# Cache attention of a decoder step: a mirrored key weight in place of eight score columns

## The chip, the cores and the metric

One core of a Trainium2 chip runs the whole program. The metric is the device time of one execution in microseconds (us), as a median over runs. PE is TensorE (PEld its weight loads), DVE is VectorE, ACT is ScalarE, POOL is GpSimd, SP is SyncE, whose queue issues most transfers.

## What is computed

One layer of a decoder for 1024 prompt tokens and 8 sequences with one new token each (decode tokens). Every decode sequence has 8192 earlier positions in a paged cache: a latent of 256 values and a rotary key of 32 values. The part that matters here, cut from the reference (`qf` is the normed query of 8 heads x 96 values, 64 of them without rotary part):

```python
def mla_keys(ckv, kpe, w_uk, g_kn):
    k_nope = jnp.einsum('btc,chd->bthd', ckv, w_uk)
    k_pe = jnp.broadcast_to(kpe[:, :, None, :], ...)
    return rms_norm(jnp.concatenate([k_nope, k_pe], axis=-1), qk_gain(g_kn))
...
k = mla_keys(ckv_blk, kpe_blk, w_uk, g_kn)
s = jnp.einsum('bqhd,bkhd->bhqk', qf, k) * scale
...
p = jnp.exp(s - m_new[..., None])
acc = acc * alpha[..., None] + jnp.einsum('bhqk,bkc->bhqc', p, ckv_blk)
```

So for each cached position two things are needed of the 8 x 64 key values k = latent x w_uk: their squares' sum per head (for the norm) and their product with the query per head (the score). The rotary part adds 32 more values, shared by the heads.

## The kernel before

The program is a row of stages, each a block in which the five engines run their own instruction streams and wait for each other on semaphores: `project_in`, `make_heads`, `attend_prompt` (attention of the prompt), `cache_and_merge` (the cache attention of the 8 sequences, then the output projection with w_o and the norm), `gate_and_up`, `down` (the MLP). Wide products are made at fp32 accuracy with three fp32r products: an operand is split into `hi` (rounded) and `lo` (rest), and hi x hi, hi x lo and lo x hi are added in PSUM.

`cache_and_merge` goes through the 8 sequences one after the other. A sequence has 64 tiles of 128 positions, taken as 32 pairs `n`. `gather` on POOL issues indirect loads, two per chunk of 8 tiles (latents of 1 MB, rotary keys), two sequences ahead. For each pair:

- PE, `turn`: four transposes of the next pair's latents into `TT`. ACT copies them as `hi` (L1498), DVE makes `lo` (L1667).
- PE, `keys` (L1306 to L1318): for each of the two tiles 6 products (2 halves of the latent, `ck`, x 3 terms) with the key weights. The weights `w_hi`, `w_lo` have 520 columns: 512 of w_uk and 8 that hold w_uk x query, so that the scores fall out beside the key values. A PSUM bank takes 512 fp32 columns, so each product is two matmuls of 260 columns, `half` 0 and 1, into two banks: 12 matmuls a tile, 24 a pair.
- ACT, `squares` (L1591): squares of the 512 key values from `KK` in PSUM into `sq` in SBUF.
- DVE, `sums`: sums of 64 squares for each head out of `sq` (L1769), then a copy of the 8 scores out of `KK` (L1771), which increments `scored`.
- `KK` has room for two tiles. `keys` of tile t waits for `scored` of tile t-2 (L1310 to L1311):

```python
for t in range(2):
    if n >= 1 or b > 0:
        pe.wait_ge(scored, b * TILES + 2 * n + t - 1)
```

The order of the work is written by hand. On PE a pair is: rotary transposes if n % 4 == 0 (`turn_rotary`), `turn(n + 1)`, `keys(n)`, rotary product if n % 4 == 1 (`rotary`). On DVE it is: `lo(n)`, at n == 24 `queries`, `sums(n - 1)`, `rotary_scores` if n % 4 == 3 (L1776, L1780), then a step of the softmax tail of the sequence before (`tail`, n = 9, 11, 13, 17, 21). On ACT: `hi(n)`, `squares(n - 1)`, `rotary_turned` if n % 4 == 0. In the last sequence ACT and DVE also split w_o (L1526, L1689) in pairs 19 to 31.

`queries` (L1647 to L1659) puts the next sequence's 8 score columns into `w_hi` and `w_lo` (4 small operations) and its rotary query into `q_pe` (1). Before the first sequence, PE multiplies w_uk with all queries (L1468, "absorbed"), ACT and DVE split the result (L1617, L1834).

## Time and profile before

| | |
|---|---|
| median of 3 runs | 2309.01 us (2308.57 to 2309.56) |
| profiled execution, own time | 2308.62 us |
| its span | 2306.8 us |
| cache stage, from the first `keys` to the last | 432 to 1382 us |
| mean granted TensorE clock | 0.984 of full |

The span is the time from the first to the last instruction of the profiled execution; its own time is 1.8 us longer and 0.4 us under the median. A row of a timeline is start, duration, engine, line, operation, output <- input, shapes, and in brackets the idle time before it with what ended it. Rows with xN are N instructions merged; then the duration runs from the first start to the last end. Matmuls are pipelined: one starts before the end of the one before it, so the spacing of starts tells their price, not their duration.

### The profile page before, as it was taken

The page shows a single profiled execution, that of the slowest core. Times are in us where ns is not written, and L with a number is a line of the kernel's source. Part 1 is how long each engine was busy: PE and PEld are TensorE (multiplying, and loading weights), DVE is VectorE, ACT ScalarE, POOL GpSimd, SP SyncE. Part 2 cuts the span into 40 slices and gives each one's busy share as a digit, 9 for nine tenths or more (in the row PEclk, how much of TensorE's full clock was granted, in tenths as well). Part 3 has the DMA queues.
Part 4 walks back from the last instruction along what each step waited for, and adds up shares of the span by engine and source line. Part 5 has one row for each costly group of instructions (what it writes and reads, how often), then busy time and mean ns, then how long its engine had stood idle before and what let it go on. Part 6 is the DMA issues. An engine that isn't in the chain of part 4 may idle for free. (4 is left out here: it accounts for less than half of the span.)

```text
span 2306.8 us, 39961 instructions
## 1 busy us (share of the span) xinstructions
PE 2240.1 (97%) x15923; PEld 2009.7 (87%) x15923; DVE 1393.4 (60%) x2663; ACT 946.9 (41%) x1788; POOL 325.5 (14%) x412
## 2 busy tenths in 40 slices
PE   8989899899999999999999999989999999999998
PEld 7965466799999999999999987769999999978776
DVE  4326677566666666666666675556767676754345
ACT  4435566455454545454545563321111111133334
POOL 2106300501212212130303112100000000000000
PEclk9989999899999999999999999999999999999999
DMA  4110000710212212030404014221111111144444
GB/s 158 48 40 0 39 19 11 291 58 1 110 57 79 88 51 116 24 142 4 163 1 174 11 55 148 75 77 46 45 45 45 45 45 45 37 140 127 165 168 134
DMA packets 93449, 180.39 MB, mean 78 GB/s; under 512 B 9048, under 2 KB 64168, under 8 KB 84927
## 3 DMA queue, kind: packets, MB, share of 16 engines
q1 hardware_dynamic: 77789, 93.65, 12.7%
q0 software_dynamic: 15504, 84.60, 9.5%
q8 instruction: 105, 1.72, 0.3%
q14 instruction: 51, 0.42, 0.1%
HBM read 164.21 MB, written 14.33 MB: 77 GB/s over the span
## 5 line engine op out<-in xcount | busy, mean ns | idle before, releaser
L1769 DVE TENSOR_REDUCE ca_cells<-ca_sq 128x8 f32<-128x512 f32 x512 | 350.8, 685 | 257.7 <-ACT ca_sq L1591 255.0
L1591 ACT ACTIVATE ca_sq<-ca_KK 128x512 f32<-128x512 f32 x512 | 306.6, 599 | 382.5 <-PE ca_KK L1315 382.4
L1315 PE MATMUL ca_KK<-ca_w_hi,ca_hi 128*128 128x260 f32 x2048 | 432.2, 292 | 1.9 <-DVE ca_cells L1771 1.5
L1315 PE MATMUL ca_KK<-ca_w_lo,ca_hi 128*128 128x260 f32 x2048 | 412.5, 283 | 0.0
L1315 PE MATMUL ca_KK<-ca_w_hi,ca_lo 128*128 128x260 f32 x2048 | 412.3, 283 | 0.0
L1315 PEld LDWEIGHTS ca_KK<-ca_w_hi,ca_hi 128*128 128x128 f32 x2048 | 313.6, 189 | 4.6 <-issue 2.8
L1315 PEld LDWEIGHTS ca_KK<-ca_w_lo,ca_hi 128*128 128x128 f32 x2048 | 316.1, 189 | 0.0
L1315 PEld LDWEIGHTS ca_KK<-ca_w_hi,ca_lo 128*128 128x128 f32 x2048 | 315.3, 189 | 0.0
L1940 PE MATMUL gu_GU<-mlp_h_hi,gu_w_hi 128*128 128x344 f32 x1056 | 225.1, 322 | 3.2 <-DVE gu_w_lo L1985 3.2
L1667 DVE TENSOR_TENSOR ca_lo<-ca_TT,ca_hi 128x512 fp32r<-128x512 f32 x256 | 175.6, 686 | 82.6 <-ACT ca_hi L1498 75.7
L1940 PE MATMUL gu_GU<-mlp_h_lo,gu_w_hi 128*128 128x344 f32 x1056 | 224.7, 321 | 0.0
L1940 PE MATMUL gu_GU<-mlp_h_hi,gu_w_lo 128*128 128x344 f32 x1056 | 223.4, 320 | 0.0
L1498 ACT ACTIVATE ca_hi<-ca_TT 128x512 fp32r<-128x512 f32 x256 | 152.7, 597 | 74.0 <-PE ca_TT L1290 73.9
L1940 PEld LDWEIGHTS gu_GU<-mlp_h_hi,gu_w_hi 128*128 128x128 f32 x1056 | 178.4, 189 | 3.3 <-DVE gu_w_lo L1985 3.3
L1940 PEld LDWEIGHTS gu_GU<-mlp_h_lo,gu_w_hi 128*128 128x128 f32 x1056 | 179.5, 190 | 0.0
L1940 PEld LDWEIGHTS gu_GU<-mlp_h_hi,gu_w_lo 128*128 128x128 f32 x1056 | 176.3, 188 | 0.0
L1290 PE MATMUL ca_TT<-keep_ident,ca_lat 128*128 128x128 f32 x1024 | 155.2, 274 | 0.9 <-issue 0.9
L2026 DVE RECIPROCAL gu_room<-gu_room 128x1032 f32<-128x1032 f32 x22 | 145.3, 6603 | 0.8
L1290 PEld LDWEIGHTS ca_TT<-keep_ident,ca_lat 128*128 128x128 f32 x1024 | 119.7, 142 | 4.2 <-issue 4.0
L1966 ACT ACTIVATE gu_room<-gu_GU 128x1032 f32<-128x1032 f32 x22 | 22.8, 1036 | 226.1 <-PE gu_GU L1940 226.1
L2171 PE MATMUL dn_OUT<-dn_w_hi,dn_g_hi 128*128 128x512 f32 x352 | 111.6, 398 | 1.2 <-DVE dn_g_lo L2230 0.3
L2227 DVE TENSOR_TENSOR dn_w_lo<-dn_raw,dn_w_hi 128x1024 fp32r<-128x1024 f32 x44 | 53.9, 1225 | 93.5 <-ACT dn_w_hi L2193 93.5
(309 smaller groups left out, 3297.9 us busy)
## 6 DMA issues: line engine op xcount, KB each, us to landing
dn_raw<-in_w_down SPq DMA_DIRECT2D x44, 512.0 KB, 3.7
keep_w_uv<-in_w_gate SPq DMA_DIRECT2D x22, 512.0 KB, 3.8
gu_up_raw<-in_w_up SPq DMA_DIRECT2D x22, 512.0 KB, 3.9
keep_ctx<-in_w_down SPq DMA_DIRECT2D x22, 512.0 KB, 3.7
late_room<-in_x_prompt SPq DMA_DIRECT2D x8, 512.0 KB, 3.7
ca_m<-mixed_scratch SPq DMA_DIRECT2D x8, 512.0 KB, 4.0
ca_w_raw<-in_w_o SPq DMA_DIRECT2D x16, 256.0 KB, 2.7
ca_x<-in_x_prompt SPq DMA_DIRECT2D x8, 512.0 KB, 3.7
```

What stands on the lines that cost most here:

```text
L1290: last = nc.tensor.transpose(TT[:, n % 2, (2 * t + ck) * P:(2 * t + ck + 1) * P], src, keep.ident[:])
L1315: last = nc.tensor.matmul(KK[:, t, half, 0:HALF], x[:, n % 2, t, ck, :], w[:, ck, half, par * (NH // 2):par * (NH // 2) + HALF], start=(m ...
L1498: nc.scalar.activation(hi[:, n % 2], TT[:, n % 2, :].rearrange("p (t c k) -> p t c k", t=2, c=2), ACT.Copy).then_inc(hi_done, 1)
L1591: nc.scalar.activation(sq[:, t], KK[:, t, :, KEYS[par]], ACT.Square).then_inc(squared, 1)
L1667: nc.vector.tensor_tensor(lo[:, n % 2], TT[:, n % 2, :].rearrange("p (t c k) -> p t c k", t=2, c=2), hi[:, n % 2].bitcast(F32), ALU.subtra ...
L1769: nc.vector.tensor_reduce(ss[:, par, 2 * n + t, :], sq[:, t].rearrange("p a (h d) -> p (a h) d", d=DN), AX.X, ALU.add).then_inc(summed, 1)
L1940: ins = nc.tensor.matmul(GU[:, 3 * kind + j, 0:F3], w[:, kind, k, :], h[:, k, j * F3:(j + 1) * F3], start=(k == 0 and n == 0), stop=(k == ...
L1966: nc.scalar.activation(gate[:, 2:2 + TOK].rearrange("p (j t) -> p j t", j=3), GU[:, 0:3, 0:F3], ACT.Copy)\
L2026: link(nc.vector.reciprocal(sig, sig))
L2171: last = nc.tensor.matmul(OUT[:, t, h, :], g[:, b, t * P:(t + 1) * P], w[:, b, h * 512:(h + 1) * 512], start=(f == 0 and k == 0), stop=(f ...
L2227: nc.vector.tensor_tensor(w_lo[:, b, :], raw[m % RING], w_hi[:, b, :].bitcast(F32), ALU.subtract).then_inc(w_lo_done, 1)
```

## The change

The 8 score columns go. For each sequence and head, the 64 columns of w_uk are multiplied by a reflection (a "mirror") that takes the first axis to the direction of the head's query. A reflection keeps the sum of squares, so the norm can be taken from the mirrored key values, and the first of them is, up to a factor `coef`, the score. Weights are then 512 columns wide, one bank, but differ from sequence to sequence.

- `keys` issues 6 matmuls of 512 columns a tile. `KK` and the new `SQ` are banks of one PSUM tensor `KS`: ACT now squares from PSUM into PSUM, DVE reduces from PSUM. The copy of the 8 scores becomes a product with `coef`, read with a step of 64.
- New per sequence: SP loads a row of 512 values, broadcast to 128 partitions (`w_row`, 256 KB, from a scratch in DRAM). DVE, `refresh`: `fresh = w_row * u`, then `fresh += w_uk`, for each of two `ck`, in pairs 20 and 22. ACT, `split_w`: `w_hi = fresh` in pairs 23 and 25. DVE, `refresh_lo`: `w_lo = fresh - w_hi` in pairs 24 and 27. `queries` keeps 1 of its 5 operations.
- New once: 9 DVE operations at the end of `make_heads` (8 partitions), which also loses the two query units (8 transposes, 2 ACT copies) at its end; 17 POOL operations and 2 stores in `attend_prompt`, 4 small ACT operations there, after items 14 and 30 of 64; 8 transposes and an ACT copy before "absorbed". Before the first sequence, `refresh`, `split_w` and `refresh_lo` of sequence 0 stand on the way; the old split of w_uk (2 ACT, 2 DVE operations) is gone.
- The rotary keys of two sequences no longer fit and lie in a ring of 12 chunks: `gather` waits on POOL for `kpe_squared` from the 5th chunk on.

```diff
@@ make_heads, DVE, at its end
+            q = keep.q_s[:, :, 0:DN]
+            big, none, ge = (keep.mirror[:, n, :] for n in (BIG, NONE, SIGN))
+            step(nc.vector.tensor_reduce(big, q, AX.X, ALU.max, apply_absolute_value=True))
...
+            step(nc.vector.tensor_reduce(keep.mirror[:, SQUARE, :], keep.w_row, AX.X, ALU.add))
@@ attend_prompt, ACT
+                if n == 14:
+                    guess_norm()
+                if n == 30:
+                    guess_inverse()
@@ places in a sequence
+FRESH_AT, HI_AT, LO_AT = (20, 22), (23, 25), (24, 27)
@@ gather, POOL
+        if b >= 1 and n >= RING - CHUNKS:
+            nc.gpsimd.wait_ge(keep.kpe_squared, (b - 1) * CHUNKS + n - (RING - CHUNKS) + 1)
@@ PSUM
-        KK = c.ps("KK", [P, 2, 2, 512])
+        KS = c.ps("KS", [P, 2, 2, 512])
+        KK, SQ = KS[:, :, 0, :], KS[:, :, 1, :]
@@ SP
+            for b in range(NB):
+                if b >= 1:
+                    sp.wait_ge(w_made, 2 * b)
+                if b >= 2:
+                    sp.wait_ge(complete, b - 1)
+                sp.dma_start(w_row, row_broadcast(keep.w_dram[b:b + 1, :], WIDE)).then_inc(w_in, 16)
@@ PE, keys
-                        for half in range(2):
-                            last = nc.tensor.matmul(KK[:, t, half, 0:HALF], x[:, n % 2, t, ck, :],
-                                                    w[:, ck, half, par * (NH // 2):par * (NH // 2) + HALF],
-                                                    start=(m == 0), stop=(m == 5))
+                        last = nc.tensor.matmul(KK[:, t, :], x[:, n % 2, t, ck, :], w[:, par, ck, :],
+                                                start=(m == 0), stop=(m == 5))
@@ ACT, squares, and the new split
-                    nc.scalar.activation(sq[:, t], KK[:, t, :, KEYS[par]], ACT.Square).then_inc(squared, 1)
+                    nc.scalar.activation(SQ[:, t, :], KK[:, t, :], ACT.Square).then_inc(squared, 1)
+            def split_w(b, ck):
+                act.wait_ge(w_made, 2 * b + ck + 1)
+                nc.scalar.activation(w_hi[:, b % 2, ck, :], fresh[:, b % 2, ck, :], ACT.Copy).then_inc(w_hi_set, 1)
@@ DVE
+            def refresh(b, ck):
+                if ck == 0:
+                    dve.wait_ge(w_in, 16 * (b + 1))
+                    if b > 1:
+                        dve.wait_ge(keyed, b * TILES - TILES)
+                new = fresh[:, b % 2, ck, :].rearrange("p (h d) -> p h d", h=NH)
+                made = nc.vector.tensor_tensor(new, w_row.rearrange("p (h d) -> p h d", h=NH),
+                                               keep.u[:, ck, b, :].unsqueeze(2).to_broadcast([P, NH, DN]), ALU.mult)
+                made.then_inc(w_step, 1)
+                dve.wait_ge(w_step, 2 * b + ck + 1)
+                nc.vector.tensor_tensor(fresh[:, b % 2, ck, :], fresh[:, b % 2, ck, :], keep.w_uk[:, ck, :], ALU.add)\
+                  .then_inc(w_made, 1)
+            def refresh_lo(b, ck):
+                dve.wait_ge(w_hi_set, 2 * b + ck + 1)
+                last = nc.vector.tensor_tensor(w_lo[:, b % 2, ck, :], fresh[:, b % 2, ck, :],
+                                               w_hi[:, b % 2, ck, :].bitcast(F32), ALU.subtract)
+                if ck == 1:
+                    last.then_inc(q_set, 1)
@@ DVE, sequence, after lo(n) and ahead of sums(n - 1)
-                    if n == 24 and b < NB - 1:
+                    if n in FRESH_AT and b < NB - 1:
+                        refresh(b + 1, FRESH_AT.index(n))
+                    if n == LO_AT[0] and b < NB - 1:
                         queries(1 - par, b + 1)
+                    if n in LO_AT and b < NB - 1:
+                        refresh_lo(b + 1, LO_AT.index(n))
@@ DVE, sums
-                    nc.vector.tensor_reduce(ss[:, par, 2 * n + t, :], sq[:, t].rearrange("p a (h d) -> p (a h) d", d=DN),
+                    nc.vector.tensor_reduce(ss[:, par, 2 * n + t, :], SQ[:, t, :].rearrange("p (h d) -> p h d", d=DN),
                                             AX.X, ALU.add).then_inc(summed, 1)
-                    nc.vector.tensor_copy(raw[:, par, 2 * n + t, :].rearrange("p (a h) -> p a h", a=2),
-                                          KK[:, t, :, SCORES[par]]).then_inc(scored, 1)
+                    nc.vector.tensor_tensor(raw[:, par, 2 * n + t, :], KK[:, t, :].rearrange("p (h d) -> p h d", d=DN)[:, :, 0],
+                                            keep.coef[:, b, :], ALU.mult).then_inc(scored, 1)
```

How the order moves, on PE, in the middle of a sequence: the first tile of a pair before (`ca_KK` are the key products, `ca_TT` the transposes of the next latents).

```order
L1290 MATMUL ca_TT<-keep_ident,ca_lat 128x128 x4
L1315 MATMUL ca_KK<-ca_w_hi,ca_hi 128x260 x2
L1315 MATMUL ca_KK<-ca_w_lo,ca_hi 128x260 x2
L1315 MATMUL ca_KK<-ca_w_hi,ca_lo 128x260 x2
L1315 MATMUL ca_KK<-ca_w_hi,ca_hi 128x260 x2
L1315 MATMUL ca_KK<-ca_w_lo,ca_hi 128x260 x2
L1315 MATMUL ca_KK<-ca_w_hi,ca_lo 128x260 x2
```

And the same tile in the changed program:

```order
L1366 MATMUL ca_TT<-keep_ident,ca_lat 128x128 x4
L1390 MATMUL ca_KS<-ca_w_hi,ca_hi 128x512
L1390 MATMUL ca_KS<-ca_w_lo,ca_hi 128x512
L1390 MATMUL ca_KS<-ca_w_hi,ca_lo 128x512
L1390 MATMUL ca_KS<-ca_w_hi,ca_hi 128x512
L1390 MATMUL ca_KS<-ca_w_lo,ca_hi 128x512
L1390 MATMUL ca_KS<-ca_w_hi,ca_lo 128x512
```

Twelve instructions of a tile have become six; the second tile of the pair follows in the same way.

On DVE of the changed program, pairs 19 to 20 of a sequence (`ca_fresh` is the new weight, `ca_cells` takes sums and scores):

```order
L1876 COPY ca_cells<-ca_KP 128x64
L1880 TENSOR_REDUCE ca_cells<-ca_kpe_sq 128x8
L1763 TENSOR_TENSOR ca_lo<-ca_TT,ca_hi 128x512
L1735 TENSOR_TENSOR ca_fresh<-keep_w_uv,attn_u 128x512
L1739 TENSOR_TENSOR ca_fresh<-ca_fresh,attn_w_uk 128x512
L1869 TENSOR_REDUCE ca_cells<-ca_KS 128x8
L1871 TENSOR_TENSOR ca_cells<-ca_KS,attn_coef 128x8
```

The two rows L1735 and L1739 are new, between `lo(20)` and the sums that release PE. In pair 22 they stand again, in pair 24 and 27 one row `ca_w_lo` (L1745) stands at that place:

```order
L1876 COPY ca_cells<-ca_KP 128x64
L1880 TENSOR_REDUCE ca_cells<-ca_kpe_sq 128x8
L1763 TENSOR_TENSOR ca_lo<-ca_TT,ca_hi 128x512
L1754 TENSOR_SCALAR ca_q_pe<-attn_q_pe 128x32
L1745 TENSOR_TENSOR ca_w_lo<-ca_fresh,ca_w_hi 128x512
```

Before, five small rows (L1654 four times, L1657) stood there in pair 24 and nothing in the others.

## Rows read from the trace of the kernel before

**Rows 1.** Windows: stretch, length, busy (x instructions) of PE, PEld, DVE, ACT, POOL, clock, DMA, GB/s.
```profile
425.20:435.40 10.20, 9.20 (x42) 8.73 (x42) 3.42 (x14) 2.71 (x7) 7.83 (x8) 0.50 1.00 395
432.00:1382.00 950.00, 948.23 (x8467) 916.98 (x8468) 610.84 (x1493) 495.80 (x929) 192.59 (x198) 1.00 0.21 81
```

**Rows 2.** Waits of PE, 440 to 1400 us: total, times, longest.
```profile
PE ca_KK L1315 <- DVE ca_cells L1771: 1.5, 2, 0.9
```

**Rows 3.** Timeline of the cache stage, a pair with its rotary product.
```profile
802.19 0.68 DVE L1667 TENSOR_TENSOR ca_lo<-ca_TT,ca_hi 128x512 fp32r<-128x512 f32 x1
...
802.55 0.40 PE L1315 MATMUL ca_KK<-ca_w_hi,ca_hi 128*128 128x260 f32 x2
...
802.75 0.60 ACT L1591 ACTIVATE ca_sq<-ca_KK 128x512 f32<-128x512 f32 x1 [0.78 <-PE ca_KK L1315]
...
803.38 0.69 DVE L1769 TENSOR_REDUCE ca_cells<-ca_sq 128x8 f32<-128x512 f32 x1 [0.51 <-ACT ca_sq L1591]
...
803.98 0.61 PE L1332 MATMUL ca_KP<-ca_q_pe,ca_kpeT 128*128 128x128 f32 x4
803.99 0.15 DVE L1771 COPY ca_cells<-ca_KK 128x8 f32<-128x8 f32 x1
...
804.43 0.60 PE L1290 MATMUL ca_TT<-keep_ident,ca_lat 128*128 128x128 f32 x4
...
804.78 0.37 PE L1315 MATMUL ca_KK<-ca_w_hi,ca_hi 128*128 128x260 f32 x1
```

**Rows 4.** Timeline of DVE, rotary scores, once in four pairs.
```profile
514.63 0.21 DVE L1776 COPY ca_cells<-ca_KP 128x64 f32<-128x64 f32 x1
...
542.50 0.21 DVE L1776 COPY ca_cells<-ca_KP 128x64 f32<-128x64 f32 x1
```

**Rows 5.** The same in the last sequence.
```profile
1336.68 0.21 DVE L1776 COPY ca_cells<-ca_KP 128x64 f32<-128x64 f32 x1
...
1381.05 0.21 DVE L1776 COPY ca_cells<-ca_KP 128x64 f32<-128x64 f32 x1
```

**Rows 6.** Chain that ended last, a stretch of w_down, 512 columns.
```profile
2048.00 85.73 PE dn_OUT L2171 x378
```

**Rows 7.** Timeline of PE, merge stage, 512 columns.
```profile
1401.17 0.63 PE L1398 MATMUL ca_KK<-ca_w_o_lo,ca_m_hi 128*128 128x512 f32 x2
...
1402.10 0.62 PE L1398 MATMUL ca_KK<-ca_w_o_hi,ca_m_hi 128*128 128x512 f32 x2
```

**Rows 8.** Timeline, pair 24, where `queries` stands.
```profile
634.33 0.68 DVE L1667 TENSOR_TENSOR ca_lo<-ca_TT,ca_hi 128x512 fp32r<-128x512 f32 x1
...
634.93 0.40 DVE L1654 TENSOR_SCALAR ca_w_hi<-attn_qa_hi 128x8 fp32r<-128x8 f32 x2
...
635.31 0.68 DVE L1769 TENSOR_REDUCE ca_cells<-ca_sq 128x8 f32<-128x512 f32 x1
...
635.90 0.15 DVE L1771 COPY ca_cells<-ca_KK 128x8 f32<-128x8 f32 x1
...
636.24 0.48 PE L1315 MATMUL ca_KK<-ca_w_hi,ca_hi 128*128 128x260 f32 x2
```

**Rows 9.** Timeline of DVE, pair 21: the context copy.
```profile
626.85 0.41 DVE L1805 TENSOR_SCALAR keep_ctx<-ca_CT 128x256 f32<-128x256 f32 x1
```

**Rows 10.** Timeline, start of the cache stage.
```profile
428.46 0.34 ACT L1617 ACTIVATE attn_qa_hi<-ca_TT 128x64 fp32r<-128x64 f32 x2 [4.27 <-PE ca_TT L1468]
...
431.78 0.80 PE L1315 MATMUL ca_KK<-ca_w_hi,ca_hi 128*128 128x260 f32 x2
```

**Rows 11.** Timeline, end of make_heads.
```profile
256.40 0.94 DVE L804 TENSOR_REDUCE attn_s_own<-hd_sq_q 8x8 f32<-8x768 f32 x1
...
260.20 1.12 ACT L729 ACTIVATE mid_mixT<-hd_T,hd_s_pool 128x344 f32<-128x344 f32 x2 [0.42 <-PE hd_T L656]
```

**Rows 12.** Tile hd_log on ACT: duration ns min/median/max, first and last start.
```profile
L691 ACT ACTIVATE hd_log<-hd_mean x9: 215/216/217, 173.1 to 249.0; 128x16 f32<-128x16 f32 x9
```

**Rows 13.** Groups by line and form, DVE before 440 us: a reduce from PSUM.
```profile
L946 DVE TENSOR_REDUCE at_nmax<-at_S 128x1 f32<-128x512 f32 x8 | 5.5, 692 | 0.3
```

More of the change, by code:

```diff
@@ L575, in make_heads @@
         UNITS = ([(i, u) for i in range(PT) for u in range(5)] + [("y", g, j) for g in range(4) for j in range(2)]
-                 + [(PT, 3), (PT, 4)] + [("y", g, 2) for g in range(4)])
+                 + [("y", g, 2) for g in range(4)])
         number = {unit: n for n, unit in enumerate(UNITS)}
@@ L842, in _ @@
                     window(i // 2)
+BIG, NONE, SIGN, SQUARE, LOG, GUESS, NORM, ARM, STEP, BETA, COEF = range(11)
 def attend_prompt(nc, io, keep):
@@ L867, in attend_prompt @@
         stored = c.sem("stored")
+        mirror_step, norm_guessed, arm_made, arm_guessed, mirror_made = (
+            c.sem("mirror_step"), c.sem("norm_guessed"), c.sem("arm_made"), c.sem("arm_guessed"), c.sem("mirror_made"))
+        row_stored, mirror_logged = c.sem("row_stored"), c.sem("mirror_logged")
+        stat = [keep.mirror[:, n, :] for n in range(COEF + 1)]
         items = [(hp, i if hp % 2 == 0 else PT - 1 - i, e) for hp in range(NH // 2) for i in range(PT)
@@ L1390, in project @@
                 else:
-                    pe.wait_ge(squared, NB * TILES - 1 + a)
                     pe.wait_ge(scored, NB * TILES - 1 + a)
@@ L1465, in _ @@
             pe.wait_ge(w_kept, 2)
+            pe.wait_ge(mirrors_kept, 1)
             for ck in range(2):
                 for h in range(NH):
-                    last = nc.tensor.matmul(A[:, ck, h, :], w_ukT[ck][:, h, :], keep.q_new[0:DN, h, :],
+                    last = nc.tensor.matmul(A[:, ck, h, :], w_ukT[ck][:, h, :], mirrorT[:, h, :],
                                             start=True, stop=True)
@@ L1511, in sequence @@
                         rotary_turned(par, b, n // 4)
+                    if b < NB - 1 and n in HI_AT:
+                        split_w(b + 1, HI_AT.index(n))
                     if b == NB - 1:
@@ L1610, in _ @@
                                      ACT.Copy).then_inc(w_kept, 1)
+            act.wait_ge(rep_turned, 1)
+            nc.scalar.activation(mirrorT, V[0:DN], ACT.Copy).then_inc(mirrors_kept, 1)
+            act.wait_ge(absorbed, 1)
+            nc.scalar.activation(keep.u[:], A.rearrange("p c h b -> p c b h"), ACT.Copy).then_inc(absorbed_kept, 1)
             for ck in range(2):
-                last = nc.scalar.activation(w_hi[:, ck, :, NH // 2:HALF], keep.w_uk[:, ck, :].rearrange("p (a n) -> p a n", a=2),
-                                            ACT.Copy)
-            last.then_inc(w_set, 1)
-            act.wait_ge(absorbed, 1)
-            for ck in range(2):
-                last = nc.scalar.activation(keep.qa_hi[:, ck, :, :], A[:, ck].rearrange("p h b -> p b h"), ACT.Copy)
-            last.then_inc(qa_hi_done, 1)
+                split_w(0, ck)
             sequences(act, sequence)
@@ L1831, in _ @@
                 last = nc.vector.tensor_copy(keep.q_pe[rows, :, s, :], B[rows].rearrange("p h b -> p b h"))
-            dve.wait_ge(qa_hi_done, 1)
-            for ck in range(2):
-                last = nc.vector.tensor_tensor(keep.qa_lo[:, ck, :, :], A[:, ck].rearrange("p h b -> p b h"),
-                                               keep.qa_hi[:, ck, :, :].bitcast(F32), ALU.subtract)
             last.then_inc(prepared, 1)
@@ L1838, in _ @@
             queries(0, 0)
+            dve.wait_ge(coef_in, 16)
+            dve.wait_ge(absorbed_kept, 1)
+            for ck in range(2):
+                refresh(0, ck)
+            for ck in range(2):
+                refresh_lo(0, ck)
             sequences(dve, sequence)
```

133 lines of the change are left out of this document (87 added, 46 removed).

## The prediction

> **What bounds the kernel now.** I read the busy time by stretch first. In the cache stage, 432 to 1382 us, PE is busy for 948 of 950 us, DVE for 611, ACT for 496 [rows 1]. Busy PE could still hide stalls, so the waits come next: in that stage PE waited for DVE's score copies 1.5 us in total, in 2 cases [rows 2]. PE's issue is therefore the bound, and the question is what a tile costs on PE. In the timeline the second tile of a pair starts at 802.55 and what follows it at 803.98 [rows 3]: 12 matmuls in 1.43 us, **0.119 us each**. Four pairs take (542.50 - 514.63)/2 = 13.94 us [rows 4]. The last sequence is the exception: three such cycles take 1381.05 - 1336.68 = 44.37 us instead of 41.8 [rows 5]; there ACT and DVE, which also split w_o, set part of the pace.
>
> The timeline also tells how near the next limit is. PE may begin the next pair's first tile when DVE has copied the scores of this pair's first. That chain is ACT's square at 802.75, the reduce at 803.38, the copy, done at 803.99 + 0.15 = 804.14. Without the rotary product (803.98 to 804.43, 0.45 us) PE would want the bank after its tile and four transposes (804.43 to 804.78, 0.35), at 803.98 + 0.35 = 804.33 [rows 3]. The slack is **0.19 us a pair**. DVE sits idle 0.51 us before that reduce; from start to start, `lo` (802.19) to reduce is 1.19 us, of which `lo` itself takes 0.60 (634.33 to 634.93), so 0.59 is spare [rows 3, 8].
>
> **The matmuls.** 12 of 260 columns become 6 of 512. Two places show 512-column fp32r matmuls with a weight load each. In the stage of w_down 378 take 85.73 us, 0.227 each [rows 6]; in the merge stage 4 take 1402.10 - 1401.17 = 0.93, 0.2325 each [rows 7]. I take 0.228, near the long stretch, because 378 matmuls weigh more than 4, and a little above it because all engines work beside. A tile then costs 6 x 0.228 = 1.368 instead of 1.428 us: 0.060 x 512 tiles = **-30.7 us**. Ends: -34.0 with 0.227, -16.9 with 0.2325.
>
> A rule speaks for less. The Trainium skill (VectorE: DVE Perf Modes, section on the TRN2 errata) prices a matmul at max(60, 6 + columns) cycles of 2.4 GHz, 0.111 us for 260 and 0.216 for 512 columns; by it a tile would fall from 1.330 to 1.295, and the estimate for the term would be -18 us. The rows contradict both prices: 0.119 and 0.227.
>
> **What shortening does to the slack.** The second tile now takes 1.37 instead of 1.43, so the slack of 0.19 becomes 0.13, as long as ACT's square into PSUM and DVE's reduce out of PSUM cost what they do now, 0.60 and 0.69. A reduce of 512 from PSUM is in the trace, 0.692 [rows 13]. A square with PSUM as destination is not: I bound it by the present 0.60 and by 0.69, the longest plain operation on 512 columns of PSUM here, and take 0.60, since source, length and function stay; at 0.69 the slack would still hold. The product with `coef` is as small as the copy it replaces. Cost taken: 0.
>
> **The new work on DVE** is where PE will stop. It stands between `lo(n)` and the sums that release PE. I take 0.69 for each 512-column operation, as for `lo` and the reduce [rows 3]; the next one starts 0.60 to 0.61 later, or 0.72 where it waits for the result. `refresh` thus adds 0.72 + 0.61 = 1.33 us, `refresh_lo` 0.61.
> - Pair 20 comes after rotary scores, as pair 24 does. Pair 24 now: `lo` 634.33, reduce 635.31, copy done 636.05, PE starts at 636.24, slack 0.19 with `queries` between [rows 8]. From `lo` to reduce it is 0.98 there; with `refresh` in place of `queries` it is 0.60 + 1.33 = 1.93. Delay 0.95, slack 0.19 less 0.12 for the shorter pair: stall 0.9.
> - Pair 22: spare 0.59 - 0.06 for the earlier square, less 0.34 of the context copy in pair 21 [rows 9], leaves 0.19; delay 1.33 - 0.19 = 1.14; slack 0.13 and the 0.45 of the rotary product: stall 0.6.
> - Pair 24: `lo` to reduce 0.60 + 0.09 + 0.61 = 1.30 instead of 0.98; delay 0.32, slack 0.07: stall 0.3.
> - Pair 27: 0.61 against 0.53 spare and 0.13 slack: 0.
> Together 1.8 us a sequence, in 7 sequences **+12.6 us**. Queued behind it on DVE are the second tile's sums and `lo` of the next pair; both have more than 0.9 us before PE needs them, so nothing is added. Ends: +6, if idle time absorbs more, +20, if pairs 21, 23 and 25 stall too.
>
> **The last sequence.** Where DVE's and ACT's chain sets the pace, a shorter tile gives nothing: 24 tiles x 0.060 = **+1.4 us** given back.
>
> **The start.** Now: absorbed at 428.46, keys at 431.78 [rows 10], 3.3 us. Afterwards, from about 428.6: ACT's copy 0.3, four DVE operations 2.8, the second split 0.6, `refresh_lo` 0.7, then PE's two rotary transposes and the four of `turn(1)`, six where four take 0.35 at full clock [rows 3], so 1.1 at the half clock granted here (0.50 from 425.20 to 435.40, its 1.2 GHz level [rows 1]): keys at 434.2, **+2.4 us**. Ends +1 and +5, the upper one if the idle PE gets its full clock later. The first broadcast row is issued at the stage's start, and I take it as landed by then; each us that it is late costs one.
>
> **The other stages.** In `attend_prompt` ACT gets four operations of 0.215 [rows 12] ahead of copies that PE waits for: **+0.8 us** (0 to 2, POOL's short operations beside DVE included). At the end of `make_heads` DVE, done at 257.34, gets four operations of 0.69 and five of 0.16 with 0.04 between, and ends at 261.3; ACT ended the stage at 261.32 and now ends earlier, without the query units [rows 11]: DVE takes its place, 0. The two `split_w` on ACT lie in the 0.78 us that it idles before a square [rows 3]: 0; without that cover they would cost 0.6 each. Loads of 256 KB a sequence, the DMA engines at 0.21 [rows 1]: 0. POOL's ring waits ask for chunks that are squared by pair 12, and its gather starts after pair 18: 0.
>
> **Sum:** -30.7 + 12.6 + 1.4 + 2.4 + 0.8 = -13.5. Against the profiled execution 2308.6 - 13.5 = 2295.1; the median lies 0.4 above it: **2295.5 us**.
>
> **Rivals.**
> - *Price by the column, slower.* 0.119/260 is 0.458 ns a column. If the time of a matmul goes by its columns, 512 cost 0.2345, and the change is what its title says, 8 columns of 520: 512 x (1.428 - 1.407) = -10.8, and the sum is +6.4: **2315.4**. It decides in every tile, from 0.2323 a matmul on (512 x (1.428 - 6x) = 17.2). For it: the merge stage's 0.2325 [rows 7]. Against it: 378 in a row at 0.227 [rows 6]. Chance 0.07. That the change does not do what it says is this case.
> - *The chain through PSUM, slower.* If square and reduce together grow by more than the 0.13 slack, PE waits once a pair: 256 x 0.1 = 25.6 us for each 0.1 beyond it. At +0.18 the gain is gone; at +0.25: -13.5 + 30.7, **2326**. Against it: the reduce row of 0.692 [rows 13]. Chance 0.05.
> - *No difference.* The merge stage's price, 0.2325, holds here: -16.9 + 17.2, **2309.3**. Chance 0.12. The skill's rule above, -18 us, would also end here.
> - *The refreshes are nearly hidden.* PE's stalls come to 0.4 us a sequence: 2295.5 - 9.8 = **2285.7**. For it: PE waited only twice now [rows 2], so the places are well chosen. Against it: 1.33 us do not fit into 0.53. Chance 0.14.
>
> **Numbers.** The forecast (2289 to 2302) has 0.62. A measurement here can tell 0.2%, 4.6 us, from no change. Faster by more: 0.62 + 0.14 = 0.76, of which I leave 0.01 to a mix of ends that falls short, 0.75; within it 0.13; slower 0.12. The range takes in the forecast, the hidden refreshes (down to 2284 with the cheaper matmul) and most of the no-difference case: 2284 to 2310.
>
> **What the next profile must show.** Spacing of the key matmuls near 0.228. A cycle of four pairs without refresh 13.94 - 8 x 0.060 = 13.46 us. PE waits for DVE's score products (L1871) about 3 a sequence, 0.3 to 0.9 us each, 12 to 13 us in total, all near pairs 20 to 24. First keys at about 434. If PE waits in every pair, the chain through PSUM is the cause; if the cycle is 13.8 and nobody waits, the price by the column.

## The result and the profile after

The changed kernel takes **2296.72 us** in the median of 5 runs (2295.01 to 2298.11) against 2309.12 for the kernel before beside it (5 runs, 2308.57 to 2309.56). The ratio is 0.9949, 95% interval 0.9937 to 0.9960: shorter by 12.4 us or 0.5%, forecast 13.5. The profiled execution takes 2296.94 us, its span is 2295.2 instead of 2306.8.

The windows of the changed kernel, with the columns of [rows 1]: the cache stage, then two short stretches of the merge stage.

```profile
434.00:1375.00 941.00, 929.95 (x5409) 751.89 (x5408) 635.65 (x1510) 498.63 (x946) 196.21 (x196) 1.00 0.22 83
1430.90:1434.30 3.40, 3.40 (x11) 2.77 (x11) 0.77 (x4) 0.00 (x0) 0.00 (x0) 0.53 0.37 146
1465.00:1468.40 3.40, 3.40 (x10) 2.67 (x9) 0.00 (x0) 0.00 (x0) 0.00 (x0) 0.53 0.32 94
```

PE is still the bound, but no longer without a gap: 929.95 of 941 us busy, where [rows 1] had 948.23 of 950. The waits of PE, 440 to 1400 us, with the columns of [rows 2]:

```profile
PE ca_KS L1390 <- DVE ca_cells L1871: 9.6, 17, 1.0
```

From 2 waits on DVE to 17, none longer than 1.0; four of the 17, 2.2 us in total, lie in the last sequence, the other 13 at the refreshes. The pair that answers to [rows 3]:

```profile
802.70 0.47 PE L1390 MATMUL ca_KS<-ca_w_hi,ca_hi 128*128 128x512 f32 x1
...
803.93 0.39 PE L1390 MATMUL ca_KS<-ca_w_hi,ca_lo 128*128 128x512 f32 x1
...
804.35 0.58 ACT L1669 ACTIVATE ca_KS<-ca_KS 128x512 f32<-128x512 f32 x1 [0.78 <-PE ca_KS L1390]
...
804.97 0.69 DVE L1869 TENSOR_REDUCE ca_cells<-ca_KS 128x8 f32<-128x512 f32 x1 [0.67 <-ACT ca_KS L1669]
...
805.52 0.60 PE L1366 MATMUL ca_TT<-keep_ident,ca_lat 128*128 128x128 f32 x4
805.58 0.15 DVE L1871 TENSOR_TENSOR ca_cells<-ca_KS,attn_coef 128x8 f32<-128x8 f32 x1
...
805.88 0.48 PE L1390 MATMUL ca_KS<-ca_w_hi,ca_hi 128*128 128x512 f32 x1
```

Its two tiles start 12 matmuls between 802.70 and 805.52: 0.235 each with the slower first ones; over all starts of the stage that follow one another without a gap the spacing is **0.2301** on average (5% under 0.224, 5% over 0.236), and that of the 260-column matmuls before was 0.1194. The rotary scores of DVE, once in four pairs as in [rows 4]; the pairs 20 to 23 lie before 515.94 and before 634.21:

```profile
501.19 0.21 DVE L1876 COPY ca_cells<-ca_KP 128x64 f32<-128x64 f32 x1
...
515.94 0.21 DVE L1876 COPY ca_cells<-ca_KP 128x64 f32<-128x64 f32 x1
...
529.76 0.21 DVE L1876 COPY ca_cells<-ca_KP 128x64 f32<-128x64 f32 x1
...
543.26 0.21 DVE L1876 COPY ca_cells<-ca_KP 128x64 f32<-128x64 f32 x1
...
556.73 0.21 DVE L1876 COPY ca_cells<-ca_KP 128x64 f32<-128x64 f32 x1
...
619.17 0.21 DVE L1876 COPY ca_cells<-ca_KP 128x64 f32<-128x64 f32 x1
...
634.21 0.21 DVE L1876 COPY ca_cells<-ca_KP 128x64 f32<-128x64 f32 x1
...
648.00 0.21 DVE L1876 COPY ca_cells<-ca_KP 128x64 f32<-128x64 f32 x1
```

Two plain cycles are 543.26 - 529.76 = **13.50** and 556.73 - 543.26 = **13.47** us; forecast was 13.46. The same two before are not alike. The first is the 13.94 of [rows 4]; the second, across the change of sequence, ends here:

```profile
556.34 0.22 DVE L1776 COPY ca_cells<-ca_KP 128x64 f32<-128x64 f32 x1
```

and takes 556.34 - 542.50 = 13.84. Place by place the change gains 0.43 and 0.37 us a cycle, not the 0.48 forecast. The cycle with the pairs 20 and 22 takes 634.21 - 619.17 = **15.04** (in the first sequence 14.75), the one with 24 and 27 takes 13.79. The last sequence, against [rows 5]:

```profile
1328.87 0.21 DVE L1876 COPY ca_cells<-ca_KP 128x64 f32<-128x64 f32 x1
...
1372.59 0.21 DVE L1876 COPY ca_cells<-ca_KP 128x64 f32<-128x64 f32 x1
```

Three cycles in 43.72 instead of 44.37 us. The start of the stage, against [rows 10]:

```profile
429.04 0.28 ACT L1697 ACTIVATE attn_u<-ca_TT 128x128 f32<-128x128 f32 x1 [6.34 <-PE ca_TT L1543]
429.41 0.69 DVE L1735 TENSOR_TENSOR ca_fresh<-keep_w_uv,attn_u 128x512 f32<-128x512 f32 x1 [6.68 <-ACT attn_u L1697]
...
432.07 1.47 DVE L1745 TENSOR_TENSOR ca_w_lo<-ca_fresh,ca_w_hi 128x512 fp32r<-128x512 f32 x2
...
433.60 0.69 PE L1398 MATMUL ca_KP<-keep_ident,ca_kpe 128*128 128x128 f32 x2 [2.98 <-DVE ca_w_lo L1745]
...
434.79 0.78 PE L1390 MATMUL ca_KS<-ca_w_hi,ca_hi 128*128 128x512 f32 x1
```

Where the 11.6 us of the span went, by the first and last key matmul and the first matmul of gate_and_up. Of the changed kernel:

```profile
1374.08 0.39 PE L1390 MATMUL ca_KS<-ca_w_hi,ca_lo 128*128 128x512 f32 x1
...
1519.10 1.23 PE L2038 MATMUL gu_GU<-mlp_h_hi,gu_w_hi 128*128 128x344 f32 x3 [3.20 <-DVE gu_w_lo L2083]
```

and of the kernel before:

```profile
1382.54 0.40 PE L1315 MATMUL ca_KK<-ca_w_hi,ca_lo 128*128 128x260 f32 x2
...
1530.30 1.23 PE L1940 MATMUL gu_GU<-mlp_h_hi,gu_w_hi 128*128 128x344 f32 x3 [3.19 <-DVE gu_w_lo L1985]
```

| stretch | before | after | |
|---|---|---|---|
| start to first key | 431.78 | 434.79 | +3.0 |
| first to last key | 950.76 | 939.29 | -11.5 |
| last key to gate_and_up | 147.76 | 145.02 | -2.7 |
| the rest of the span | 776.5 | 776.1 | -0.4 |

### The profile page after: what moved, and what is told of

It is laid out like the page before. It is cut to its first block and busy times, and to the rows that moved or that the text cites. A ratio compares the mean times of both kernels' runs of the same rounds, so it can differ in the third digit from the quotient of the medians.

```text
span 2295.2 us, 33888 instructions
## 1 busy us (share of the span) xinstructions
PE 2213.6 (96%) x12851; PEld 1838.7 (80%) x12851; DVE 1423.1 (62%) x2684; ACT 948.1 (41%) x1804; POOL 337.1 (15%) x431
## 5 line engine op out<-in xcount | busy, mean ns | idle before, releaser
L1869 DVE TENSOR_REDUCE ca_cells<-ca_KS 128x8 f32<-128x512 f32 x512 | 352.9, 689 | 221.2 <-ACT ca_KS L1669 217.6
L1669 ACT ACTIVATE ca_KS<-ca_KS 128x512 f32<-128x512 f32 x512 | 297.9, 582 | 368.0 <-PE ca_KS L1390 366.8
L1390 PE MATMUL ca_KS<-ca_w_hi,ca_hi 128*128 128x512 f32 x1024 | 423.7, 414 | 10.9 <-DVE ca_cells L1871 9.6
L1390 PE MATMUL ca_KS<-ca_w_hi,ca_lo 128*128 128x512 f32 x1024 | 403.3, 394 | 0.0
L1390 PE MATMUL ca_KS<-ca_w_lo,ca_hi 128*128 128x512 f32 x1024 | 401.3, 392 | 0.0
L1390 PEld LDWEIGHTS ca_KS<-ca_w_hi,ca_hi 128*128 128x128 f32 x1024 | 192.8, 188 | 53.9 <-issue 17.2
L1390 PEld LDWEIGHTS ca_KS<-ca_w_hi,ca_lo 128*128 128x128 f32 x1024 | 192.5, 188 | 44.0
L1390 PEld LDWEIGHTS ca_KS<-ca_w_lo,ca_hi 128*128 128x128 f32 x1024 | 193.5, 189 | 30.7
```

The source lines that it names most:

```text
L1390: last = nc.tensor.matmul(KK[:, t, :], x[:, n % 2, t, ck, :], w[:, par, ck, :], start=(m == 0), stop=(m == 5))
L1669: nc.scalar.activation(SQ[:, t, :], KK[:, t, :], ACT.Square).then_inc(squared, 1)
L1869: nc.vector.tensor_reduce(ss[:, par, 2 * n + t, :], SQ[:, t, :].rearrange("p (h d) -> p h d", d=DN), AX.X, ALU.add).then_inc(summed, 1)
```

## Experiments

Each kernel is compared with the kernel before on its own chip. Cycles are those of the rotary scores. e1, e2, e3 and e7 shared a chip on which the kernel before took 2306.84 us (2303.23 to 2309.73) and the changed kernel was not run; against the changed kernel, stretches of the traces are compared, since medians of two chips differ by some us of their own.

**e1_spread: the same work on DVE, one operation a pair.** The two operations of each refresh are set apart.

```diff
-FRESH_AT, HI_AT, LO_AT = (20, 22), (23, 25), (24, 27)
+MULT_AT, ADD_AT, HI_AT, LO_AT, QUERIES_AT = (19, 23), (22, 25), (23, 26), (27, 30), 26
...
-                    if n in FRESH_AT and b < NB - 1:
-                        refresh(b + 1, FRESH_AT.index(n))
...
+                    if n in MULT_AT and b < NB - 1:
+                        refresh(b + 1, MULT_AT.index(n))
+                    if n in ADD_AT and b < NB - 1:
+                        refresh_add(b + 1, ADD_AT.index(n))
```

> The six DVE operations that make the next sequence's weights stand one by one in pairs 19, 22, 23, 25, 27 and 30 instead of two by two in 20 and 22 and singly in 24 and 27. My account (PE stops because 1.33 us of DVE work do not fit into about 0.53 us of spare time and 0.13 of slack, while 0.61 us do): the stalls of about 1.9 us a sequence go, 7 x 1.9 = 13.3 us, so 2283.5 us, and the four-pair cycles around pairs 20 to 27 fall from 15.06 and 13.81 to 13.5. Rival, the amount of DVE work counts and not its place: 2296.7, nothing changes. Rival, single operations still overrun by some tenths each: 2288 to 2292.

2285.22 us (2283.35 to 2288.41), ratio 0.9910 (0.9896 to 0.9923). PE's waits and two cycles of the second half of a sequence:

```profile
PE ca_KS L1390 <- DVE ca_cells L1876: 2.2, 4, 1.0
```
```profile
617.66 0.22 DVE L1881 COPY ca_cells<-ca_KP 128x64 f32<-128x64 f32 x1
...
631.12 0.21 DVE L1881 COPY ca_cells<-ca_KP 128x64 f32<-128x64 f32 x1
...
644.78 0.21 DVE L1881 COPY ca_cells<-ca_KP 128x64 f32<-128x64 f32 x1
```

The cycle of the pairs 20 to 23 is 13.46 instead of 15.04, that of 24 to 27 is 13.66 instead of 13.79. The four waits left lie in the last sequence. So the stall was the place of the refresh, two operations in one pair, and not the work: the idle time of DVE takes one operation of 0.69 a pair, not two. One of the six single operations, the addition in pair 25, still costs 0.2: from the keys of pair 24 to those of 25 it takes 0.22 longer than in e3, the next experiment, on average over six sequences, and all other such steps agree within 0.04.

**e3_one_mirror: no refresh at all.** All sequences use the mirrored weights of the first; refresh, split and their loads are left out for the other seven.

```diff
-            for b in range(NB):
+            for b in range(1):
...
-                        last = nc.tensor.matmul(KK[:, t, :], x[:, n % 2, t, ck, :], w[:, par, ck, :],
+                        last = nc.tensor.matmul(KK[:, t, :], x[:, n % 2, t, ck, :], w[:, 0, ck, :],
...
-                    if n in FRESH_AT and b < NB - 1:
-                        refresh(b + 1, FRESH_AT.index(n))
```

> As the changed kernel, but all sequences use the first sequence's mirrored weights: the refresh, split and lo operations and the broadcast loads of sequences 1 to 7 are left out. My account: PE's stalls in pairs 20 to 27 all come from them, 7 x 1.9 = 13.3 us, so 2283.5 us, with all four-pair cycles at 13.5 outside pairs 8 to 19. Rival, the stalls have another source (PSUM bank shared with the squares, the product in place of the copy): part of them stays, 2288 to 2296.

2287.08 us (2284.13 to 2288.47), ratio 0.9911 (0.9896 to 0.9926), the same as e1. From the first to the last key it takes 926.75 us, 12.5 under the changed kernel. The price of the refreshes, forecast as 12.6 and read from the cycles as about 13, is thus shown from a second side. Pair by pair, on average over six sequences, PE starts the keys late, compared with e3, by 0.99 us in pair 20, 0.62 in 22, 0.34 in 24 and 0.00 in 27; forecast were 0.9, 0.6, 0.3 and 0. e1 takes 927.76 us from first to last key, so it gets 11.5 of the 12.5 back while doing the work.

**e2_halves: 512 columns in two matmuls.** The last five of six products of a tile are issued as 2 x 256 columns.

```diff
-                        last = nc.tensor.matmul(KK[:, t, :], x[:, n % 2, t, ck, :], w[:, par, ck, :],
-                                                start=(m == 0), stop=(m == 5))
+                        for cols in (slice(0, 512),) if m == 0 else (slice(0, 256), slice(256, 512)):
+                            last = nc.tensor.matmul(KK[:, t, cols], x[:, n % 2, t, ck, :], w[:, par, ck, cols],
+                                                    start=(m == 0), stop=(m == 5 and cols.stop == 512))
```

> As the changed kernel, but of the six 512-column matmuls of a tile the last five are issued as two of 256 columns each, 11 matmuls a tile. The columns are the same, the count is not. My account: a matmul of 260 took 0.1194 us and one of 512 takes 0.2301 here; with 0.4167 ns a column at 2.4 GHz that is 11 and 17 ns above the columns. Two of 256 then cost 2 x 0.1177 = 0.2354 against 0.2301: 5 x 0.0053 x 512 = +13.6 us, 2310. Rival, price by the column alone: +0, 2296.7. Rival, a fixed 11 ns for each instruction whatever its width: +28 us, 2325.

2318.56 us (2317.38 to 2320.25), ratio 1.0053 (1.0037 to 1.0068): slower than before, and from the first to the last key 960.0 us, 20.7 over the changed kernel. A plain cycle:

```profile
543.48 0.21 DVE L1877 COPY ca_cells<-ca_KP 128x64 f32<-128x64 f32 x1
...
557.33 0.21 DVE L1877 COPY ca_cells<-ca_KP 128x64 f32<-128x64 f32 x1
```

13.85 instead of 13.47, 0.38 over 8 tiles x 5 splits, 0.0095 a split. The same comes out of the spacings: 2 x 0.1198 - 0.2301 = 0.0095. So there is a price of an instruction beside that of its columns. Price by the column, the forecast's first rival, would have left the time alone; it falls. The expectation's own account, 0.0053 a split and +13.6 us, was too small by a third to a half.

**e7_no_scores: before, without the eight columns.** 12 matmuls of 256 columns; the scores are left out (the copy reads key columns in their place).

```diff
-                            last = nc.tensor.matmul(KK[:, t, half, 0:HALF], x[:, n % 2, t, ck, :],
-                                                    w[:, ck, half, par * (NH // 2):par * (NH // 2) + HALF],
+                            last = nc.tensor.matmul(KK[:, t, half, 0:4 * DN], x[:, n % 2, t, ck, :],
+                                                    w[:, ck, half, NH // 2:HALF],
...
-                                          KK[:, t, :, SCORES[par]]).then_inc(scored, 1)
+                                          KK[:, t, :, 0:NH // 2]).then_inc(scored, 1)
```

> The kernel before, with its 8 score columns left out: 12 matmuls of 256 columns a tile instead of 260, everything else alike (the scores are copied from key columns). It measures what the columns alone are worth. My account: 12 x 4 x 0.4167 ns x 512 tiles = -10.2 us, 2299.0 us, four-pair cycle 13.93 - 0.16 = 13.77. Rival, the matmul of 260 is not bound by its columns but by its weight load: no change, 2309.

2294.98 us (2294.62 to 2295.22), ratio 0.9949 (0.9934 to 0.9964). A plain cycle, in a place where the kernel before has 13.94:

```profile
513.64 0.21 DVE L1776 COPY ca_cells<-ca_KP 128x64 f32<-128x64 f32 x1
...
527.32 0.21 DVE L1776 COPY ca_cells<-ca_KP 128x64 f32<-128x64 f32 x1
```

13.68 against 13.94: four columns less bring the spacing from 0.1194 to 0.11725, or 0.5 ns a column, and 12 x 0.00215 x 512 = 13 us. The expectation of 10 was too small. Leaving out eight score columns alone is worth as much as the whole change, halves kept: of the 0.052 a tile that the change gained in spacing, 0.026 come from the columns (12 x 0.00215) and 0.026 from six instructions less (6 x (2 x 0.11725 - 0.2301)). In e2 the same 256 columns are spaced 0.1198. Why they cost 0.0025 more there is open: they stand between 512-wide ones, and both halves go to one PSUM bank, where e7 and the kernel before alternate between two; no run separates these. The share of 0.026 for the six instructions holds the change of banks too, and by e2's price of 0.0095 it would be 0.057.

**e5_more1 and e5_more3: how much slack has the chain?** One and three extra products of 8 columns on DVE a tile, ahead of the product that releases PE.

```diff
+                    for q in range(3):
+                        nc.vector.tensor_tensor(junk[:, t, q, :], KK[:, t, :].rearrange("p (h d) -> p h d", d=DN)[:, :, 0],
+                                                keep.coef[:, b, :], ALU.mult)
```

> The changed kernel with one more 128x8 product on DVE per tile, ahead of the scored product that releases PE (written to a tile nobody reads; work is added, nothing left out). A small operation of this kind takes about 0.08 us from start to start. Theory (in a plain pair the chain square, reduce, scored product ends 0.15 us before PE needs the bank): 0.08 lies inside that slack, so the plain four-pair cycle stays 13.47 to 13.54 us, only the waits near pairs 20 to 24 grow by 0.08 to 0.16 each; time +1 to +4 us over the changed kernel. Rival (the chain through PSUM already sets the pace, matmuls merely look slower): every pair stretches by 0.08 to 0.16, +20 to +40 us, cycle 13.8 or more.

> The same with three extra products per tile, 0.24 us ahead of the scored product. Theory (slack 0.13 to 0.15 a pair): 0.09 to 0.11 us of stall in each of 256 pairs, about +25 us, four-pair cycle 13.47 + 0.4 = 13.9, and larger stalls at the refreshes (+3 us): +25 to +32 us over the changed kernel. PE waits on the scored product many times, each short. If the slack is 0.25 or more, the plain cycle does not move and the time rises by under 8 us; if there is none, the stall is 0.24 or more a pair and the time rises by over 60 us.

On their chip (before: 2433.47) they took 2392.81 us, ratio 0.9831 (0.9812 to 0.9849), and 2424.73, 0.9965 (0.9952 to 0.9978); that chip is the subject of the next paragraphs, so the cycles decide. The plain cycle is 13.46 to 13.54 in the changed kernel on both kinds of chip, some 13.59 with one product, 13.89 with three. Two pairs of e5_more3, a plain one and one after the rotary product:

```profile
544.58 0.60 PE L1367 MATMUL ca_TT<-keep_ident,ca_lat 128*128 128x128 f32 x4
544.64 0.30 DVE L1873 TENSOR_TENSOR ca_junk<-ca_KS,attn_coef 128x8 f32<-128x8 f32 x3
...
544.86 0.16 DVE L1875 TENSOR_TENSOR ca_cells<-ca_KS,attn_coef 128x8 f32<-128x8 f32 x1
...
545.16 0.47 PE L1391 MATMUL ca_KS<-ca_w_hi,ca_hi 128*128 128x512 f32 x1
...
548.46 0.60 PE L1367 MATMUL ca_TT<-keep_ident,ca_lat 128*128 128x128 f32 x4
...
548.82 0.47 PE L1391 MATMUL ca_KS<-ca_w_hi,ca_hi 128*128 128x512 f32 x1
```

From the transposes to the next keys it is 545.16 - 544.58 = 0.58 in the plain pair and 548.82 - 548.46 = 0.36 in the other. That is the pattern throughout: in two of four pairs 0.36 becomes 0.43 with one product and 0.57 with three, 0.07 each, which is what a product takes from start to start ((544.86 - 544.64) / 3). The first one already costs in full by the distances; the cycle grows by 0.10 instead of 2 x 0.07, which would leave 0.02 of slack. The slack is therefore **zero to 0.02**, not 0.13: DVE's release ended at 544.86 + 0.16 = 545.02, PE started at 545.16, and these 0.14 us from the end of a release to PE's start are part of the chain. In the changed kernel and in e5_more3, at the pairs where PE waited for nothing but this release, it is 0.146 to 0.148. The kernel before had it too, 0.147 in the two waits of its last sequence, so it could have been read there. The theory of e5_more1 falls, that of e5_more3 holds in size (0.40 a cycle) for the wrong reason: half of the pairs pay, each the double.

**Another kind of chip: a1_after, b1_before, e1b_spread, e1c_spread.** On the chip of the e5 runs and of e1b_spread the kernel before takes 2433.5 us, on a third chip 2434.2. The third one ran the changed kernel and the kernel before themselves.

> The changed kernel itself, as the mark for the next three on one chip. On the chip of the second call every kernel, the one before among them, took 5% longer: the PE of the spread version stood still twice a sequence for 7.6 and 13 to 16 us while POOL issued its indirect loads (cycles of 21.1 and 26 to 29 us in place of 13.5), and the ratio was 0.981 instead of 0.991. If this chip has no such stalls: ratio to before 0.994 to 0.996 as at first. If it has them: the stalls are of fixed length for each kernel, so the saving of the change stays some 13 us unless before stalls longer; a ratio under 0.990 says that before's stalls are longer.

> The kernel before, for its profile on this chip. Theory: without gather stalls, cycles of four pairs of 13.85 to 13.94 us as first read. With gather stalls, the two long cycles a sequence should together be 5 to 6 us longer than in the changed kernel, because before issues its rotary keys without the ring's wait and so has more loads in one burst; rival: they are as long as in the changed kernel (within 1 us), and the greater saving comes from somewhere else, such as the granted clock.

> The spread version again, as the mark that e6 is compared with on the same chip. Theory: 0.991 of before, as measured the first time; the refresh stalls in pairs 20 to 24 stay away (four-pair cycles of 13.46 to 13.54 us). The ratio should fall into 0.989 to 0.993; beyond that, what was put down to spreading came from the runs' clock periods.

> The spread version beside the changed kernel on one chip. Theory: PE's stalls at the refreshes (1.94 us a sequence in 7 sequences, less 0.3 that remain) go: 10 to 13 us under a1_after, cycles 13.46 to 13.69 in pairs 20 to 27 instead of 15.06 and 13.81. Rival (other runs' clock periods made it): within 3 us of a1_after.

| | us | ratio (95%) |
|---|---|---|
| a1_after | 2379.36 | 0.9778 (0.9765 to 0.9791) |
| e1c_spread | 2378.26 | 0.9771 (0.9758 to 0.9784) |
| e1b_spread, on the chip of e5 | 2388.86 | 0.9814 (0.9800 to 0.9827) |

Here the change saves 55 us. All cycles but one are those of the first chip; the one in which POOL issues its 16 indirect loads is much longer. Of the kernel before, then of the changed one:

```profile
646.53 0.21 DVE L1776 COPY ca_cells<-ca_KP 128x64 f32<-128x64 f32 x1
...
676.94 0.21 DVE L1776 COPY ca_cells<-ca_KP 128x64 f32<-128x64 f32 x1
```
```profile
637.73 0.21 DVE L1876 COPY ca_cells<-ca_KP 128x64 f32<-128x64 f32 x1
...
662.55 0.21 DVE L1876 COPY ca_cells<-ca_KP 128x64 f32<-128x64 f32 x1
```

30.41 us instead of 13.8, and 24.82 instead of 15.0. The six such cycles sum to 181.4 in b1_before and 152.0 in a1_after: 29.4 us of the saving, 4.9 a sequence where 5 to 6 were expected. Another 11.9 come from the start: a burst of loads lies there too, and from the first key to the first rotary scores it takes 41.2 us in b1_before and 29.3 in a1_after, against 13.2 and 12.4 on the first chip. (The other long cycle, 21.1, which I had counted as a stall in the expectations, holds the context products and is as long on the first chip.) What happens inside, in the changed kernel (columns of [rows 1]):

```profile
650.00:660.00 10.00, 4.64 (x19) 3.73 (x18) 4.10 (x8) 2.15 (x5) 2.91 (x3) 0.83 0.98 401
```

and in its timeline:

```profile
647.42 0.40 PE L1390 MATMUL ca_KS<-ca_w_hi,ca_lo 128*128 128x512 f32 x1
...
655.31 0.58 ACT L1669 ACTIVATE ca_KS<-ca_KS 128x512 f32<-128x512 f32 x1 [5.06 <-issue]
```

DMA runs at 401 GB/s. The last matmul of a tile starts at 647.42 and ACT squares it at 655.31, 7.9 us later, where in the quiet pair above it is 0.4 (803.93 to 804.35). ACT ended a copy at 650.25 and then stood still for 5.06 us; the matmuls of the tile were done, and so were the reduces that free its place in `SQ`, so the profile shows nothing that it waited for. DVE then waited for this square and PE for DVE. On the first chip the same loads run at the same rate and nothing is late:

```profile
630.00:640.00 10.00, 9.89 (x50) 8.06 (x51) 7.19 (x19) 5.31 (x12) 4.24 (x5) 1.00 1.02 423
```

So instructions whose inputs are ready start late while the indirect loads run, on these chips and not on the other. A second loss follows: after PE has stood still, its granted clock falls to 1.2 GHz, in the kernel before and in the changed one:

```profile
654.70:671.70 17.00, 9.22 (x41) 8.85 (x42) 4.57 (x11) 4.06 (x8) 5.63 (x6) 0.50 0.81 338
```
```profile
656.40:659.80 3.40, 2.97 (x7) 2.42 (x8) 1.65 (x5) 0.79 (x3) 0.00 (x0) 0.50 0.95 398
```

Over the six long cycles PE waited 71.5 us in b1_before, and worked 49.1 us at the lower level, half of which, 24.6, is an estimate of what the clock cost: 96 of the 98.2 us by which they are longer than on the first chip. In a1_after PE waited 53.8 us, 6.7 of them at the refreshes as on the first chip, and worked 25.2 us at the lower level: 47.1 + 12.6 = 60 of 61.7. So a burst costs the kernel before 16.4 us and the changed one 10.3; of these 6.1 some 4 are shorter waits and 2 are clock. Why ACT stands still on these chips, and why PE waits longer in the kernel before, is **open**; each chip was seen at one time only, so it may be a state of theirs and not their kind. Fewer loads of instructions (81 against 105 packets of their queue in the whole program) came to mind; but no packet of an instruction queue starts between 640.75 and 669.21 in the trace of a1_after, and the 5.06 us in which ACT stands lie within. My own theory, the ring's wait on POOL, falls: POOL issues its 16 loads in 20 us in both.

And e1's gain is gone here (1.1 us between a1 and e1c, less than either's spread): its six long cycles sum to 157.3 us, 5.3 more than those of a1. PE waits 51.7 us in them, about as long as in a1 without any refresh stall of its own, and spends 72 us at the lower clock instead of 34. That the stall of pair 20 is hidden in the burst fits this, and is not shown; that the rest was lost to the clock is read from the two traces, and bursts of one kernel differ by some 2 us. The expected 10 to 13 us came out only on the chip without these stalls, and e1b_spread's ratio lies outside the 0.989 to 0.993 expected.

**e6_spread_start and e6b_spread_start: the first wait of PE, six transposes later.**

```diff
-                    if n == 0:
-                        pe.wait_ge(q_set, b + 1)
...
+                    if n == 0:
+                        pe.wait_ge(q_set, b + 1)
```

> The spread version (e1) and one wait of PE moved: for the second weight halves of the first sequence, PE waited ahead of its rotary transposes and the next pair's transposes; now only ahead of the first key matmul, so six transposes run at the half clock while DVE still splits. Theory (the start is a chain of DVE's refreshes, split, then PE): the six transposes took about 1.1 us of that chain (from 433.60 to 434.79 in the changed kernel), so first keys come 0.5 to 1.2 us earlier measured from PE's last absorbed transpose, everything after is unchanged, and the time is 0.5 to 1.2 us below that of e1 in the same call. Rival (DVE is the only bound of the start, PE would have stood idle anyway, or the transposes delay lo(0) and squares): first keys within 0.2 us of e1's distance, the same time.

> The spread version with PE's wait for the first weights moved behind six transposes, on the same chip as e1c. On the chip with stalls this could not be read: the first keys waited for lo(0) either way. Theory: first keys 0.5 to 1.2 us earlier, counted from the start of the last absorbed product's group, time 0.5 to 1.2 us below e1c. Rival: nothing, within 0.3 us in the distance. The interval of the medians (about 0.1%, 2 us) can't tell the two; the distance in the trace does.

2386.32 beside 2388.86 for e1b, and 2380.65 beside 2378.26 for e1c: no difference, ratios 0.9801 (0.9788 to 0.9815) and 0.9779 (0.9765 to 0.9792). The transposes moved ahead as meant, but the first keys did not: in e6b the first turn starts at 430.20 and the keys at 436.81, 6.6 us; in e1c 5.9. A burst of loads lies over this start too, and PE then idled 4.24 us. (Between e6 and e1b, both on the other chip, it is 8.7 and 7.9 us.) **Inconclusive** for the chip without the stalls, where it was not tried.

## Why the prediction was right, step by step

The sum was -13.5, measured -12.4 by the medians and -11.7 between the profiled executions. Each term:

- **The matmuls, -30.7: direction right, size too large.** The price of 512 columns was 0.2301, not 0.228, and that of 260 was 0.1194, not 0.119. A tile costs 6 x 0.2301 = 1.381 instead of 1.433: 0.052 x 512 = -26.7. The table of stretches gives -11.5 - 13.0 - 0.6 = -25.1 for it, without the two terms below. Of the 1.6 between, some 1.4 lie in pairs 4 to 11 of the later sequences, whose cycles gained 0.23 to 0.40 instead of 0.42. In pair 3 PE had a short wait already: ACT works on the norms of the sequence before there and squares late. The keys of pair 3 follow those of pair 2 after 3.49 us in both kernels, so a shorter tile gives nothing. The forecast took 4 matmuls of the merge stage for its price, 0.2325 [rows 7]; over all of that stage that follow without a gap it is 0.2286, so both stages were cheaper than the cache stage turned out to be. Why a matmul costs 3 ns more there than in w_down [rows 6] is not shown, but 1% of one price was 4 us of the sum. The Trainium skill's rule, weighed before (VectorE: DVE Perf Modes, section on the TRN2 errata, max(60, 6 + columns) cycles), gives as an estimate 0.109, 0.111 and 0.216 us for 256, 260 and 512 columns and -18 us for the term; the traces have 0.1173 (e7_no_scores), 0.1194 (before) and 0.2301 (after) and do not agree with any of the three prices. Its -18 misses by 8.7, my -30.7 by 4.0. The form, columns and a fixed part, is what e2 and e7 show.
- **The refresh stalls, +12.6: right.** 15.04 - 13.47 + 13.79 - 13.47 = 1.9 in six sequences and 1.6 in the first (14.75), +13.0 in all, and e3 shows 12.5. The forecast had 0.9 + 0.6 + 0.3 + 0, and e3 has 0.99 + 0.62 + 0.34 + 0 by pairs, so the mechanism is right in its parts.
- **The slack of 0.19, then 0.13: wrong, without effect on the sum.** It left out the 0.14 to 0.15 us between the end of DVE's release and PE's start. 0.19 - 0.14 - 0.06 is about zero, as e5_more1 and e5_more3 show. The term of the chain through PSUM was put at 0 and is 0, but by luck, with 0.02 to spare at most: the square costs 0.582 into PSUM instead of 0.599, and the reduce 0.689. Had the square been at its upper bound of 0.69, two of four pairs would have paid 0.1, an estimate of some 13 us, where the forecast wrote that the slack would still hold. The rival "chain through PSUM" had deserved more than 0.05.
- **The last sequence, +1.4: 0.6.** It gained 44.37 - 43.72 = 0.65 in three cycles where a plain cycle gained 0.4 each: about half was given back, not all.
- **The start, +2.4, and attend_prompt, +0.8: together 3.2, measured 3.0, but shared otherwise.** The cache stage began 0.4 earlier than before, so attend_prompt cost nothing that was left at its end, and the start cost 3.4. The copy L1697 came at 429.04, not 428.6, as the absorbed product before it took 6.16 us instead of 5.22, with the clock at 1.2 GHz from 423.7 on instead of 425.2; DVE's chain from 429.41 to PE's transposes at 433.60 was as forecast. Keys at 434.79 instead of 434.2.
- **The other stages, 0: missed -2.7.** The merge stage is not touched by the change and became shorter. TensorE's clock is at 1.2 GHz there in two stretches. In the kernel before, with the columns as above:

```profile
1438.90:1445.70 6.80, 6.80 (x22) 5.53 (x22) 1.14 (x4) 0.00 (x0) 0.00 (x0) 0.50 0.19 69
1473.10:1479.90 6.80, 6.21 (x18) 4.92 (x19) 0.54 (x1) 0.00 (x0) 0.00 (x0) 0.50 0.40 133
```

Twice 6.8 us at the lower level, in the changed kernel twice 3.4. 6.8 us less at half speed are up to 3.4 us of work, enough for the gain of 2.7. The profile of e1_spread has one such stretch of 6.8 us in its merge stage and that of e2_halves two, with the same code in this stage, so it is no gain of the change to count on. They take 143.4 and 147.4 us from the last key to gate_and_up, the changed kernel 145.0 and the kernel before 147.8.

So the sum is nearer to the result than its terms are, by luck: the matmuls gave 5.6 us less than forecast, and 2.7 of these came back from the clock of a stage that the change does not touch. Without that the span would have shrunk by some 9 us.

Of the signs named ahead, the spacing (0.228, measured 0.230), the plain cycle (13.46, measured 13.47 to 13.50, though the gain is smaller, since the 13.94 it was counted from holds in some places and 13.84 in others) and the first keys (434, 434.8) came as said. The waits of PE at the refreshes came to 7.4 us in 13 cases (9.6 in 17 less the last sequence's 2.2 in 4) instead of 12 to 13 in 21. The cycles hold 13.0; that the modelled ends of the matmuls cover the first tenths of each stall would explain it, and is not shown. Of the rivals, the price by the column falls with e2, the nearly hidden refreshes with e3 (12.5 us and not 2.8), and no difference with the spacing of 0.2301 against the 0.2325 it needed.
